# Start addresses in SBUF: a shared region moved by 32 bytes, and three of its tensors moved further

## What is computed

```python
# first block (one layer; its context is not updated)
y = sigmoid(gate_a) * (y_a @ w_br_attn) + sigmoid(gate_d) * (y_d @ w_br_dn)
x = x + gt1 * (y @ w_out)                                  # "merge" and "out1"
x = x + gt2 * square(relu(norm(x) @ w_mlp1)) @ w_mlp2      # perceptron m0
# second block, layers l = 0 and 1
mix = concat(pool_mixer(u), head_out(diff_attn(q, k, v)))
x = x + ga * (mix @ w_out)
x = x + gm * square(relu(norm(x) @ w_mlp1)) @ w_mlp2       # perceptrons m1 (l = 0), m2 (l = 1)
# the same for the 256 context rows, in layer l = 0 alone
```

## Time and profile before

| | |
|---|---|
| runs | 2679.93, 2682.19, 2685.24 us (median 2682.19) |
| span of the profiled execution | 2676.4 us |
| PE busy | 2521.2 us, 94% |
| PEld busy (weight loads, beside PE) | 2039.4 us, 76% |
| DVE busy | 1557.1 us, 58% |
| ACT busy | 931.9 us, 35% |
| POOL busy | 115.6 us, 4% |
| chain that ended last | PE 85%, DVE 9%, issue 3%, ACT 2%, DMA 1% |
| mean granted TensorE clock | 0.978 of full speed |

### The profile page before, as it was taken

The page is one execution under the profiler, slowest core; times in us unless marked ns, Lnnn a source line. Parts: engine busy times, 40 slices in busy tenths (PEclk is TensorE's granted clock), DMA queues, the critical chain, the costliest instruction groups (busy, mean ns, idle before and its releaser), DMA issues.

```text
span 2676.4 us, 45804 instructions
## 1 busy us (share of the span) xinstructions
PE 2521.2 (94%) x19622; PEld 2039.4 (76%) x19622; DVE 1557.1 (58%) x2412; ACT 931.9 (35%) x1599; POOL 115.6 (4%) x222
## 2 busy tenths in 40 slices
PE   6999988779999999999998999999999998999997
PEld 3777667667887788877777888888887776788886
DVE  3355577767656788854675556545445466534444
ACT  3344443223235223342553432222233254422322
POOL 0000001120100010000000000000000000000000
PEclk8999899989999999999999999999999999999999
DMA  6000000004653555411002123333321102222210
GB/s 277 32 32 1 33 3 4 5 5 172 221 214 118 181 189 190 172 44 59 5 32 79 64 95 126 126 126 126 126 95 44 63 32 86 93 97 103 95 63 32
DMA packets 32202, 244.88 MB, mean 91 GB/s; under 512 B 3616, under 2 KB 3776, under 8 KB 20992
## 3 DMA queue, kind: packets, MB, share of 16 engines
q1 hardware_dynamic: 11808, 164.83, 15.4%
q0 software_dynamic: 20192, 77.11, 9.1%
HBM read 239.83 MB, written 2.10 MB: 90 GB/s over the span
## 4 chain that ended last, share of the span: by engine, by line
PE 85%; DVE 9%; issue 3%; ACT 2%; DMA 1%; POOL 0%; DVEq 0%; SPq 0%; ACTq 0%
PE ps L337 57%; PE ps L2190 2%; PE ps L2419 2%; PE ps L949 1%; PE ps L2447 1%; PE ps L1370 1%; PE ps L2463 1%; PE ps L905 1%; PE ps L367 1%; PE ps L2465 1%; PE ps L2464 1%; PE ps L368 1%; PE ps L369 1%; PE ps L950 1%; PE ps L951 1%
## 5 line engine op out<-in xcount | busy, mean ns | idle before, releaser
L337 PE MATMUL ps<-hh,ws 128*128 128x512 f32 x3216 | 752.9, 393 | 10.9 <-DVE hh L524 7.1
L337 PEld LDWEIGHTS ps<-hh,ws 128*128 128x128 f32 x3216 | 601.3, 188 | 144.9 <-issue 15.6
L318 ACT ACTIVATE ws<-raw 128x1024 fp32r<-128x1024 f32 x295 | 308.6, 1049 | 430.0 <-PE ps L337 396.6
L326 DVE TENSOR_TENSOR ws<-raw,ws 128x1024 fp32r<-128x1024 f32 x295 | 359.8, 1221 | 151.5 <-ACT ws L318 151.4
L337 PE MATMUL ps<-g,ws 128*128 128x512 f32 x1536 | 364.4, 396 | 0.0
L337 PEld LDWEIGHTS ps<-g,ws 128*128 128x128 f32 x1536 | 286.4, 188 | 66.6
L337 PE MATMUL ps<-gg,ws 128*128 128x512 f32 x960 | 227.6, 398 | 2.1 <-ACT ws L318 2.1
L1807 DVE SCALAR_TENSOR_TENSOR xT<-ps,mods,xT 128x512 f32<-128x512 f32 x120 | 90.0, 750 | 227.8 <-PE ps L337 220.5
L337 PEld LDWEIGHTS ps<-gg,ws 128*128 128x128 f32 x960 | 181.3, 189 | 46.4 <-ACT ws L318 2.5
L1970 DVE TENSOR_TENSOR sq<-sq 128x512 f32<-128x512 f32 (+1 forms) x128 | 80.0, 625 | 142.4 <-ACT sq L1947 142.4
L1947 ACT ACTIVATE sq<-ps 128x512 f32<-128x512 f32 (+1 forms) x128 | 69.4, 542 | 258.7 <-PE ps L337 244.6
(11 more groups left out here) (378 smaller groups left out, 3571.1 us busy)
## 6 DMA issues: line engine op xcount, KB each, us to landing
raw<-in_w_m SPq DMA_DIRECT2D x32, 2048.0 KB, 7.8
raw<-in_w_ada POOLq DMA_DIRECT2D x80, 512.0 KB, 3.9
raw<-in_w_mlp SPq DMA_DIRECT2D x16, 2048.0 KB, 8.0
ar<-in_w_ada POOLq DMA_DIRECT2D x48, 512.0 KB, 3.9
raw<-in_w_in SPq DMA_DIRECT2D x8, 2048.0 KB, 7.4
raw<-in_w_mg SPq DMA_DIRECT2D x8, 1536.0 KB, 7.3
raw<-in_w_out SPq DMA_DIRECT2D x6, 2048.0 KB, 8.1
raw<-in_w SPq DMA_DIRECT2D x5, 2048.0 KB, 7.5
```

Source lines behind the costliest of these rows:

```text
L318: e.activation(w_of(n)[0], pieces[n][2], ACT.Copy).then_inc(*hi(n))
L326: e.tensor_tensor(l, pieces[n][2], h.bitcast(F32), ALU.subtract).then_inc(*lo(n))
L337: m = e.matmul(o, a, b, start=n == 0, stop=n == 3 * kt - 1)
```

## The change

A tensor `line` of 32 bytes, which nothing reads or writes, is declared ahead of the shared region. Inside the region three gaps are laid: 64 bytes before `yy`, 32 before `hc2` (and so before `ctx2` behind it), and 256 before a new tensor `g3`, which takes the place of `g2` in the last perceptron m2.

```diff
         mi = sb("mi", [P, 8])
+        sb("line", [P, 8])
         REST = 18432
...
         ar, = region([("ar", [P, REST], F32)])
         hc1, = region([("hc1", [P, 2, KT, TC], F32R)])
-        gg, yy = region([("gg", [P, 2, KT, T], F32R), ("yy", [P, 2, KT, T], F32R)])
-        ar2, hc2, ctx2 = region([("ar2", [P, REST - 6144], F32), ("hc2", [P, 2, KT, TC], F32R),
-                                 ("ctx2", [P, KT, TC], F32)])
+        gg, _, yy = region([("gg", [P, 2, KT, T], F32R), ("before_yy", [P, 16], F32), ("yy", [P, 2, KT, T], F32R)])
+        ar2, _, hc2, ctx2 = region([("ar2", [P, REST - 6144], F32), ("before_hc2", [P, 8], F32),
+                                    ("hc2", [P, 2, KT, TC], F32R), ("ctx2", [P, KT, TC], F32)])
         g2, gc2 = region([("g2", [P, 2, KT, T], F32R), ("gc2", [P, 2, KT, TC], F32R)])
+        _, g3 = region([("before_g3", [P, 64], F32), ("g3", [P, 2, KT, T], F32R)])
...
-            rows_ = [(0, hh, g2, xT, T, SQX, 7)] + ([] if last else [(1, hc2, gc2, ctx2, TC, SQC, 6)])
+            rows_ = [(0, hh, g3 if last else g2, xT, T, SQX, 7)] + ([] if last else [(1, hc2, gc2, ctx2, TC, SQC, 6)])
```

## The result

The changed kernel took 2667.86 us (median of 4 runs, 2661.93 to 2670.06), the kernel before beside it 2681.78 us: a ratio of 0.9954, 95% interval [0.9939, 0.9968], so by the ratio 12.3 us less, within 8.6 and 16.4. The forecast was 17.5 us less, and the time lies inside the range.

What follows compares the result with a forecast made beforehand. The prediction took TensorE as the bound: number of matmuls by the step between them, slower where a start lies 32 bytes past a multiple of 64. Its terms summed to -17.5 us, giving 2664.7 us, range 2654 to 2674.

Steps and rivals of the forecast that it cites:

- Terms 1 and 2: `gg` in m0 and `g3` for `g2` in m2: 768 matmuls each fall by 6.56 ns, -5.04 us each.
- Term 3: `gg` in the merge: 192 matmuls fall by 6.0 ns, -1.15 us.
- Term 4: `yy`: 192 matmuls fall by 6.56 ns, -1.26 us.
- Rival A: Wide matmuls: a finer rule than 64 bytes; `yy` and `g3` gain nothing (2671.0 us) or more (2658); chance 0.15.
- Term 5: `g2` in m1, in turn with the context: 768 matmuls fall by 5.0 ns, -3.84 us.
- Term 6: Context, 256 columns: 0 for `gc2` and `hc2`; bounds -5.2 to +5.1 us and -7 to +7.
- rival B: Context matmuls on new places of `gc2` and `hc2` cost 12 us (2677) or reach the floor (2653); chance 0.06.
- Term 7: Other readers of the region: L2447, with weights in `ar2`, gains 3 ns in each of 416 matmuls, -1.2 us.
- Rival C: Whole region: slow for another reason than the start, so no change, 2682.2 us; chance 0.09.
- rival D: Wide moving reads: the place of the 2048-byte crossing sets the step, +17.6 us, 2700; chance 0.04.

Runs made afterwards that it cites:

- region_128: The kernel before with 160 unused bytes ahead of the region and no other gap, operands 128 past a multiple of 256 from `ws`: 2681.72 us, ratio 1.0009.
- weights_too: The kernel before with 32 unused bytes ahead of `ws`, so `ws`, `hh` and the region move together and all distances stay: 2679.15 us, ratio 0.9999.

## Why the prediction was right, and where not

Right in range and in place. Each term, as measured between starts in the two first profiles:

- *Terms 1 and 2*, `gg` in m0 and `g3`: -5.04 us each forecast; stretches of 44.80 became 43.52, 768 x 6.67 = -5.1 each.
- *Term 3*, the merge: -1.15 forecast, -1.3 measured (192 x (233.3 - 226.7)).
- *Term 4*, `yy`: -1.26 forecast, 192 x (233.3 - 229.0) = -0.8. Rival A's weaker side, for this tensor and not for `g3`: the finer rule exists, and its period is 256, so `g3` at 256 is whole and `yy` at 64 is not.
- *Term 5*, `g2` in m1: -3.84 forecast, 32 x 0.13 = -4.2.
- *Term 6*, the context, forecast at 0: the tiles moved, `hc2` by -1.3 us in all (some 940 matmuls by 1.46 ns) and `gc2` by +0.8 (768 by 1.1). The bounds held them, and rival B was a real mechanism, a sixth of its ceiling in size for `gc2` and of the other sign for `hc2`.
- *Term 7*, L2447 at -1.2: nothing. The 3 ns against L2432 did not go with the start, and they were a difference of durations, which overlap in a stream; the step between starts was 113.1 ns before and after. Why the two lines differ was not tested.
- `hh`, which was to stay everywhere: between context tiles it fell from 5.48 to 5.46 us, some 0.7 us in m1's 32 tiles. What stands beside a tile counts a little too.

Together the measured terms 1 to 7 make some -17 us. In the first profile 1.4 us went at layer 1's start and 7.5 before the merge, and it came to -8.1; in the second the 1.4 went too, but only 1.5 before the merge, and it came to -14.4. That the terms make nearly the 17.5 of the forecast is partly luck: term 7 and half a microsecond of `yy`, 1.7 us in all, did not come, and the other terms brought 1.1 us more than forecast. The measured 12.3 and 15.3 us are below the terms by 2 to 5 us; in the two profiles these lie where the clock differs, and how they are made up in the medians is not shown.

The step that failed is in the reading of what bounds the kernel: "a matter of how both reads stand to steps of 64 bytes, or to each other". The sum then went by the first half. `region_128` and `weights_too` show the second half to be the truth, with a period of 256 bytes. The forecast was right only because the change took the region to a whole multiple of 256 from the weights, a case which both readings price alike. By its own rule a region 128 bytes past such a multiple would have done as well, and `region_128` gains nothing; that the smallest step, 32 bytes, was one that fits is luck. The prediction noted that `gg` and `g2` came to share `hh`'s distance, in rival A, and that is what carried it. L2190 was read rightly: there too it is the distance that differs. Rival C is refuted (the time moved); rival D too, since the stretch fell to 43.52 us.

Two slips of the prediction changed nothing in the forecast. In rival B the tail of the last matmul at the earlier trace rows is not 0.4 us: the group of 96 has (10.83 - 10.67) = 0.16, and (5.52 - 0.16) / 48 gives the 111.7 ns that it wants. In its chances "half of B" is counted whole: half would give faster 0.84 and same 0.12.

The 16-byte lines of the Trainium skill's "SBUF — State Buffer", section "Specifications (TRN2)", taken alone would have had no difference between 0 and 32; the streams show 226.7 against 233.3 ns.

## What to carry to other kernels

Where one float32r stream is slower than another of the same shape, compare the starts of its two operands, modulo 256 bytes and against each other: on this chip 512-column matmuls with a weight load each ran at 226.7 ns at distance 0 and at up to 234.3 at other multiples of 32 bytes. Keep both starts on multiples of 32, for at distance 0 with both on 16 it was 231.3. Let the declarations place operands, test a rule with a case in which its readings differ, and take the price of mixed widths from a mixed stream. A difference between two profiles in a stretch where the clock falls now and then is worth a second profile of both before it is given a cause; even then small differences stay open.

## What the runs showed of the hardware

- In streams of float32r matmuls with a weight load each, starts on multiples of 32 bytes, the step depended on the distance of the two operands' starts modulo 256 bytes: 226.7 to 234.3 ns at 512 columns and 113.3 to 120.0 at 256 in steps of 32 bytes (off that grid 130.2, for 256 columns at 104 bytes; one pair at distance 160 read 120.0 and 117.3); at 128 columns it was 111.7 ns at all four distances tried. With both starts at 16 bytes a 512-column matmul took 231.3 ns at distance 0. No stream of 512 columns came under 226.7 ns.
- The best distance for one width is not that of another: 0 is the fastest at 512 columns and among the slowest at 256. Between tiles of 512 columns, a 256-column tile was fastest at 112 (8.23 us for the pair of tiles, against 8.35 at 0), of the seven distances tried.
- The same program took 343.5 and 350.1 us from the first matmul of L1183 (315.21 and 315.06 us) to the same `gg` tile (658.67 and 665.12 us) in two profiles, at a granted clock of 0.94 and 0.90 in 318 to 612 us. What decides where the clock falls was not tried.
